# A retention stage's decay tables multiplied by VectorE instead of GpSimd, a half block of matmuls placed between two transposes of a delta-rule recurrence, and one more softmax pair normalised by VectorE

## The reference, cut to what matters

```python
# first block, layer 0: gated delta rule (stage "A"), 8 heads, chunks of 64
o = gated_delta_rule_chunked(q, k, v, g, beta)
o = rmsnorm(o, out_norm) * silu(z)
y = o.reshape(...) @ w_out

# first block, layer 1: sliding window attention with sinks (stage "B"), 16 heads of 64
p = softmax(concatenate([s, sink], axis=-1))[..., :-1]
o = einsum("bnhgqk,bnkhd->bnqhgd", p, vv)
y = o.reshape(...) @ w_out + b_out

# second block (stage "R"), 8 retention heads (dk 64, dv 128) beside 8 latent attention heads
fwd = _retention_dir(q, k, v, lg_f, inclusive=True)      # gamma_f ** (i - j), j <= i
bwd = flip(_retention_dir(flip(q), flip(k), flip(v), lg_b, inclusive=False))
y_ret = _head_group_norm(fwd + bwd, gn_w)
y_ret = (silu(rg) * y_ret) @ w_ret_out
```

## Time and profile before

| | |
|---|---|
| median of 3 runs | 1445.02 us (1444.6 to 1445.6) |
| the profiled execution, its own time | 1445.35 us |
| its span, first to last instruction | 1443.5 us |
| PE busy | 1436.2 us (99%) |
| DVE busy | 1089.4 us (75%) |
| ACT busy | 772.5 us (54%) |
| POOL busy | 111.9 us (8%) |
| granted TensorE clock | full, mean 1.00 |

### The profile page before, as it was taken

How to read it: one execution, slowest core, us unless ns; L and a number is a source line. 1 busy time by engine, 2 the same in 40 slices (tenths; PEclk the granted TensorE clock), 3 DMA queues, 4 the chain that set the end, 5 groups by cost and what they waited for, 6 DMA issues and landing times.

```text
span 1443.5 us, 25372 instructions
## 1 busy us (share of the span) xinstructions
PE 1436.2 (99%) x10042; PEld 1299.7 (90%) x10042; DVE 1089.4 (75%) x1357; ACT 772.5 (54%) x1032; POOL 111.9 (8%) x113
## 2 busy tenths in 40 slices
PE   9999999999999999999999999999999999999998
PEld 7888899999888888888898988889999999988887
DVE  7887579887787757887567788756867797788853
ACT  7544458845545444544368554444756564555433
POOL 0000020020100000000013100003013001200001
PEclk9999999999999999999999999999999999999999
DMA  9564576402556456654661555457553344656461
GB/s 326 180 204 153 171 231 188 147 32 88 175 188 205 158 177 201 206 178 156 201 228 60 196 183 176 162 178 251 165 184 115 105 146 149 203 177 200 140 203 66
DMA packets 243422, 247.30 MB, mean 171 GB/s; under 512 B 6032, under 2 KB 240544, under 8 KB 243344
## 3 DMA queue, kind: packets, MB, share of 16 engines
q1 hardware_dynamic: 242096, 243.75, 51.9%
q0 software_dynamic: 960, 2.14, 0.5%
q10 hardware_dynamic: 288, 0.32, 0.1%
HBM read 245.14 MB, written 1.05 MB: 171 GB/s over the span
## 4 chain that ended last, share of the span: by engine, by line
PE 97%; ACT 1%; DVE 1%; issue 1%; ACTq 0%
PE ps L366 39%; PE ps L367 20%; PE ps L371 4%; PE ps L370 3%; PE ps L372 3%; PE ps L2476 2%; PE ps L2477 2%; PE ps L2478 2%; PE ps L579 2%; PE ps L580 1%; PE ps L1573 1%; PE ps L2075 1%; PE ps L2502 1%; PE ps L2077 1%; PE ps L2076 1%
## 5 line engine op out<-in xcount | busy, mean ns | idle before, releaser
L323 DVE TENSOR_TENSOR wlo<-raw,whi 128x2048 fp32r<-128x2048 f32 (+3 forms) x263 | 528.7, 2039 | 66.8 <-ACT whi L311 66.5
L366 PE MATMUL ps<-u,whi 128*128 128x512 f32 x1584 | 555.4, 395 | 0.0
L311 ACT ACTIVATE whi<-raw 128x2048 fp32r<-128x2048 f32 (+3 forms) x257 | 432.7, 1720 | 49.4 <-PE ps L367 43.7
L367 PE MATMUL ps<-u,wlo 128*128 128x256 f32 x1584 | 446.3, 282 | 0.0
L366 PEld LDWEIGHTS ps<-u,whi 128*128 128x128 f32 x1584 | 297.6, 188 | 67.8
L366 PE MATMUL ps<-h,whi 128*128 128x512 f32 x858 | 300.5, 394 | 0.0
L367 PEld LDWEIGHTS ps<-u,wlo 128*128 128x128 f32 x1584 | 299.4, 189 | 0.1
L367 PE MATMUL ps<-h,wlo 128*128 128x256 f32 x858 | 241.3, 281 | 0.0
L366 PEld LDWEIGHTS ps<-h,whi 128*128 128x128 f32 x858 | 161.3, 188 | 36.9
L367 PEld LDWEIGHTS ps<-h,wlo 128*128 128x128 f32 x858 | 162.0, 189 | 0.0
L678 ACT ACTIVATE gate_a<-gate_s 128x512 f32<-128x512 f32 x54 | 34.1, 632 | 235.7 <-DVE gate_s L691 235.7
(11 more groups left out here) (473 smaller groups left out, 2319.5 us busy)
## 6 DMA issues: line engine op xcount, KB each, us to landing
raw<-in_ffn_w_gu SPq DMA_DIRECT2D x85, 1024.0 KB, 5.7
raw<-in_ffn_w_down SPq DMA_DIRECT2D x32, 768.0 KB, 5.6
raw<-in_w_in SPq DMA_DIRECT2D x22, 1024.0 KB, 5.2
raw<-in_ffn_w_down SPq DMA_DIRECT2D x32, 640.0 KB, 4.2
raw<-in_a_w_in SPq DMA_DIRECT2D x16, 1024.0 KB, 6.2
raw<-in_w_ffn_gate SPq DMA_DIRECT2D x11, 1024.0 KB, 5.3
raw<-in_w_ffn_up SPq DMA_DIRECT2D x11, 1024.0 KB, 6.7
raw<-in_b_w_in SPq DMA_DIRECT2D x6, 1024.0 KB, 7.6
```

What stands on the lines that cost most here:

```text
L311: nc.scalar.activation(whi[:, s, 0:n], raw[:, s, 0:n], ACT.Copy).then_inc(w_hi, 1)
L323: ins = nc.vector.tensor_tensor(wlo[:, s, c], raw[:, s, c], whi[:, s, c].bitcast(F32), ALU.subtract)
L366: nc.tensor.matmul(o, whi[:, s, w], both, start=(first and k == 0), stop=False)
L367: ins = nc.tensor.matmul(o[:, 0], wlo[:, s, w], both[:, 0], start=False, stop=(last and k == nk - 1))
```

## The change

Three parts. (1) In stage A the half product of block 1 is cut in two: `out_turn(0, 1)`, 12 matmuls, `out_turn(1, 1)`, 12 matmuls; the second four heads of block 0 are then done with their high terms first (which need `oh`) and the low terms after (which need `ol`). (2) In stage B pair 6 joins pair 0 on DVE, and in turn 7 DVE copies the turned pair 5 before it takes the denominator of pair 6. (3) In stage R the eight multiplications of the decay tables leave POOL and stand in DVE's program in front of each head's scores.

```diff
@@ a_pe
             out_turn(0, 1)
+            pe.wait_ge(w_lo, MORE + gd + 2)
+            out_part(1, [0], range(0, half))
             out_turn(1, 1)
-            pe.wait_ge(w_lo, MORE + gd + 2)
-            out_part(1, [0, 1], range(0, half))
+            out_part(1, [1], range(0, half))
+            pe.wait_ge(sa["oh"], 4)
+            for b in range(2):
+                for k in range(half, KB):
+                    w = slice(k * WIDE + b * P, k * WIDE + b * P + P)
+                    nc.tensor.matmul(ps[:, b0 + b, tok], whi[:, s0, w], hhi[:, k, tok], start=False, stop=False)
+                    nc.tensor.matmul(ps[:, b0 + b, tok], wlo[:, s0, w], hhi[:, k, tok], start=False, stop=False)
             pe.wait_ge(sa["ol"], 4)
-            out_part(0, [0, 1], range(half, KB)).then_inc(w_used, 1)
+            for b in range(2):
+                for k in range(half, KB):
+                    w = slice(k * WIDE + b * P, k * WIDE + b * P + P)
+                    ins = nc.tensor.matmul(ps[:, b0 + b, tok], whi[:, s0, w], hlo[:, k, tok], start=False, stop=(k == KB - 1))
+            ins.then_inc(w_used, 1)
...
@@ stage B
+        BY_DVE = (0, 6)
@@ b_pool
-            for j in range(1, PAIRS):
+            for j in range(PAIRS):
+                if j in BY_DVE:
+                    continue
                 pool.wait_ge(sbn["r"], 2 * j + 2)
+                pool.wait_ge(sbn["pp"], j + 1)
...
@@ b_dve
+            def copied_turn(j):
+                dve.wait_ge(sbn["pt"], j + 1)
+                if j >= 2:
+                    dve.wait_ge(sbn["o"], j - 1)
+                nc.vector.tensor_copy(b_pt[:, j % 2, 1], ps[:, 3, 0:BS]).then_inc(sbn["ptd"], 1)
...
+                if i == 7:
+                    copied_turn(i - LAG)
                 if 1 <= i <= PAIRS:
...
-                    if j == 0:
-                        dve.wait_ge(sbn["r"], 2)
+                    if j in BY_DVE:
+                        dve.wait_ge(sbn["r"], 2 * j + 2)
+                        if j:
+                            dve.wait_ge(sbn["pp"], j + 1)
                         for t in range(2):
...
@@ r_pool
-            def head_decay(h):
-                pool.wait_ge(sr["wx"], h + 2)
-                nc.gpsimd.tensor_tensor(r_W[:, h % 2, :, QT], r_W[:, h % 2, :, QT], r_e[:, :, QT], ALU.mult).then_inc(sr["w"], 1)
-
-            head_decay(0)
-            for h in range(1, RH):
-                head_decay(h)
@@ r_dve
             def decayed_scores(h):
+                dve.wait_ge(sr["wx"], h + 2)
+                nc.vector.tensor_tensor(r_W[:, h % 2, :, QT], r_W[:, h % 2, :, QT], r_e[:, :, QT], ALU.mult).then_inc(sr["w"], 1)
                 dve.wait_ge(sr["s"], h // 2 + 1)
                 if h == 0:
                     dve.wait_ge(sr["pad"], 2)
```

More of the change, by code:

```diff
@@ L2312, in b_dve @@
                     nc.vector.reciprocal(b_r[:, pair], b_den[:, pair]).then_inc(sbn["r"], 1)
-                    if j == 0:
-                        dve.wait_ge(sbn["r"], 2)
+                    if j in BY_DVE:
+                        dve.wait_ge(sbn["r"], 2 * j + 2)
+                        if j:
+                            dve.wait_ge(sbn["pp"], j + 1)
                         for t in range(2):
-                            part = b_p[:, 0, :, Q_PARTS[t]]
-                            ins = nc.vector.tensor_tensor(part, part, b_r[:, 0:2, t].unsqueeze(2).broadcast_to(list(part.shape)),
+                            part = b_p[:, j % 3, :, Q_PARTS[t]]
+                            ins = nc.vector.tensor_tensor(part, part, b_r[:, pair, t].unsqueeze(2).broadcast_to(list(part.shape)),
                                                           ALU.mult)
@@ L2321, in b_dve @@
                     output_low(i - LAG - 1)
[L2322 to L2327, removed]
+                if LAG <= i < PAIRS + LAG and i != 7:
+                    copied_turn(i - LAG)
                 if i == 7:
```

## The result

| | before | after |
|---|---|---|
| median | 1445.03 us (22 runs, 1444.38 to 1445.86) | 1446.83 us (22 runs, 1445.96 to 1448.02) |
| profiled execution, own time | 1445.35 us | 1447.38 us |
| its span | 1443.5 us | 1445.6 us |

The ratio is 1.0013 with a 95% interval of 1.0008 to 1.0019: slower by 1.8 us, clear of the noise, and within the 0.2% that the prediction called no change. The forecast was 1446.9 us.

The account below looks back on a forecast made before the run. PE's one long program was taken to bound the kernel. Stage A -0.07, stage B 0 and stage R +1.93 sum to +1.86 us, on a median of 1445.02 giving 1446.9 us; range 1444.3 to 1448.6 us.

Parts of the forecast that it names:

- What bounds the kernel: Whole kernel: PE, busy 99% of the span, bounds it; all the change could win is well under 1 us.
- Stage A: Between the last two turns: PE's 0.40 us gap filled, then a 0.25 us wait for ACT's rounded outputs; gain 0.07 us.
- Stage B: Pair 6 on DVE: PE 0.3 to 0.4 us early, lead spent at pair 7's outputs; gain 0, bounds 0 and 0.4.
- third rival: Stages R and B: without POOL, DVE's stalls go and B's 0.4 us lead stays; 1444.9 us, chance 0.06.
- Stage R: Tables on DVE, 0.96 us each: PE 0.12 us late at heads 1, 3 and 5, 1.93 us in all at head 7.
- The hiding place for head 6: Stage R, before the split at 1122.47: 0.83 us of DVE idle time cuts its lateness to 0.93 us.
- Freed interface: Stages R and B: DVE's 1.57 us stall beside POOL goes behind head 5, B gives 0.4; 1444.9 us, chance 0.06.
- Hidden work: Stage R: DVE's idle time takes all eight multiplications, A and B give 0.3 us each; 1444.4 us, chance 0.12.
- Slower beyond doubt: Stage R: multiplication longer than 1.16 us, sum passes +2.9 us; 1448.2 us at 1.222 us; chance 0.20.

Follow-up runs that it names:

- a_short: Kernel before with only stage A's edit, 3 matmuls instead of 12 between the last two turns: 1444.43 against 1445.00 us, ratio 0.9993.
- r_odd: Kernel before with stage R's multiplications moved to DVE for heads 1, 3 and 5 only: 1446.32 against 1445.00 us, ratio 1.0008.
- r_only: Kernel before with only stage R's edit, all eight decay tables on DVE in front of the scores: 1447.17 against 1445.21 us, ratio 1.0014.
- r_even: Kernel before with stage R's multiplications moved to DVE for heads 0, 2 and 4 only: 1444.68 against 1444.92 us, ratio 0.9999.
- r_mixed: Kernel before with all eight tables on DVE, heads 1 to 5 in front of the projected block's exit from PSUM: 1446.05 against 1445.00 us, ratio 1.0008.
- a_only: Kernel before with only stage A's edit, as in the change: 1445.28 against 1445.21 us, ratio 1.0001.

## Why the prediction was right, step by step

**What bounds the kernel** held: PE's program, with a win of at most some tenths of a microsecond in reach and the loss decided by where DVE is late.

**Stage A** (forecast -0.07, measured -0.06). The gap of 0.40 went as forecast, and the wait for ACT's rounded outputs came as forecast (0.26). Not in the sum was the 0.11 us by which the matmul behind a waited one starts late as well; in its place the additional switch between transposes and matmuls, put at 0.08, cost almost nothing (its steps, +0.09, -0.08, -0.09 and +0.08, cancel). That the fit is this good is partly luck too. a_short shows why the gain was given back: with a filler of 3 matmuls the second turn is early enough, and 0.39 us stay.

**Stage B** (forecast 0, measured +0.01). The lead of 0.38 us and its loss within the next 5 us are both as forecast, but most of it (0.23) goes one step earlier in DVE's row than the forecast said, at the low part and not at the copy behind it. That DVE's row behind the denominator of pair 7 takes it back is read from the trace, where that row kept its times; no run shortened that row. It could be shortened: the half split in it takes 2.08 us beside POOL's pair 7, where most splits of 1024 columns take 1.22. The third rival's wish for a shorter row of DVE in stage B would thus have needed pair 7 off POOL, and no run tries that.

**Stage R** (forecast +1.93, measured +1.95) is right in mechanism, place and sum, but its terms were mis-sized in both directions. The multiplication was put at 0.96 and takes 0.95 us, but it holds the scores up by 1.04, since the next instruction waits for its end; the forecast used 1.0. Heads 1, 3 and 5 were put at 0.12 us each and cost 0.28: 0.17 of waiting, and 0.11 for the late second matmul. DVE's own lateness at head 7 was put at 1.93 and is 2.24 (1132.24 - 1129.91 - 0.09), because it enters head 5 already 0.57 us late and not 0.24. Head 7's step was put at 1.57 on top of the earlier ones and costs 1.39, as PE is itself 0.85 us late by then and not 0.36. And "behind it PE's program has no listed wait in which it could be given back" was wrong: the list gives idle time between records, and as matmul records overlap, the late start at 1167.07 is not in it; 0.27 us come back there. The errors, +0.49, -0.18 and -0.27, nearly cancel. Each group of steps was 0.2 to 0.5 us off; that the total fits to 0.02 us is partly luck.

**The hiding place for head 6**: the forecast took the idle time before the split as absorbing lateness unless ACT is late too, and checked ACT there. r_odd shows that this check matters: with the lateness in front of the projected block the 0.83 us absorb nothing. In the change itself DVE is late by about 1.05 us in front of that block and by about 2.1 behind it; ACT's high part moves only with the first (it ends at 1123.58), the split starts at 1123.76, and so the idle time takes the rest, as forecast.

**Freed interface**: the stall of 1.57 us went, at head 0, into idle time, as written. The rival fell. r_only and r_even show both sides: in r_only the successor of L2875 takes 0.43 us, and where POOL still multiplies head 1 (r_even), a DVE instruction is still stalled.

**Hidden work**, the second likeliest of the rivals, is true for heads 0, 2 and 4 (r_even) and for 1, 3 and 5 if they stand elsewhere (r_mixed), and false for heads 1, 3 and 5 in front of their scores (0.28 us each) and at head 7, the place without slack.

**Slower beyond doubt** needed a multiplication of more than 1.16 us. It takes 0.95 and holds the scores up by 1.04.

## What to carry to other kernels

Work moved to an engine with a quarter of its time idle costs what its place in that engine's order makes it cost: look for the closed rows, those stretches where the engine has no idle time up to something that the bottleneck waits for, and put the work in front of an idle gap that the bottleneck ends. Idle time that another engine ends absorbs lateness only if that other engine is not late for the same reason. A filler on the bottleneck should be as long as the gap that it fills and no longer, if what stands behind it starts the chain that the bottleneck needs next.

## What the runs showed of the hardware

- In every pass of `head_output` whose first matmul had to wait for its semaphore (heads 1, 3, 5 and 7 of the change), the second matmul is 0.11 us late as well: the 12 matmuls span 1.36 us up to the next one, and 1.25 to 1.26 us without a wait. In a_only the same 0.11 us stand behind the wait of 0.26.
- A DVE instruction with two inputs in SBUF that was issued while POOL's multiplication of two inputs in SBUF ran is held up until POOL is done: it takes 1.99 us before and 1.96 us in r_even, where unstalled ones of the same shape take 0.42 and 0.43 us, and it ends 0.29 and 0.30 us behind POOL's. The half split of stage B, issued 0.04 us behind the start of POOL's second multiplication of pair 7, takes 2.08 us before and 2.07 after, against 1.22 for most of that size. The other way round DVE is not slowed: a whole split that runs already takes 2.29 us with POOL's multiplication issued beside it and 2.27 to 2.29 in the change's stage R without, and it is POOL's that gets longer (3.13 us in r_odd, where it was issued 0.83 us into a split, against 1.85 at best before).
- Stretches of this PE-bound program that an edit leaves alone repeat to 0.04 us between executions whose times differ by 1 to 2 us, so a single trace resolves what ten timed runs do not. Each kernel was traced once; the repeats are between kernels that share the stretch.
